# First projections as sums of three float32r products, four more places for the experts' weights, and a changed order of late loads

## What is computed

```python
sh1, sc1, g1, sh2, sc2, g2 = adaln_params(c, w_mod[l], b_mod[l])       # silu(c) @ w_mod + b_mod, in 12 parts of 512
hx = modulate(rms_norm(x, norm1_g[l]), sh1, sc1)                       # 512 tokens
hc = modulate(rms_norm(ctx, norm1_g[l]), csh1, csc1)                   # 256 context tokens
split(h @ w_in)  # q (512), f (512), b (512), v (512), gate, aq (512), ak and av (256), ...: the projections
...              # a gated recurrence over q, f, b, v in both directions; attention over aq, ak, av; mixing; x + g1 * y
aff = softmax(h @ w_router); gate, idx = top_k(aff.T, 64)              # each of 16 experts picks 64 tokens
hid = silu(h[idx] @ w_gate) * (h[idx] @ w_up); ye = (hid @ w_down) * gate
x = x + g2 * scatter_add(ye)
```

## Time and profile before

| | us |
|---|---|
| median of 3 runs | 1913.41 (1909.41 to 1919.11) |
| the profiled execution's own time | 1913.68 |
| its span, first to last instruction | 1912.4 |
| PE busy | 1721.0 (90%) |
| DVE busy | 796.1 (42%) |
| ACT busy | 570.9 (30%) |
| read from and written to DRAM | 322.83 MB and 4.20 MB |

### The profile page before, as it was taken

How to read it: one execution, slowest core, us unless ns; L and a number is a source line. 1 busy time by engine, 2 the same in 40 slices (tenths; PEclk the granted TensorE clock), 3 DMA queues, 4 the chain that set the end, 5 groups by cost and what they waited for, 6 DMA issues and landing times.

```text
span 1912.4 us, 20334 instructions
## 1 busy us (share of the span) xinstructions
PE 1721.0 (90%) x8150; PEld 1123.7 (59%) x8150; DVE 796.1 (42%) x1325; ACT 570.9 (30%) x1026; POOL 117.2 (6%) x123
## 2 busy tenths in 40 slices
PE   5989899886999996998888888999888899999999
PEld 2656667564877773333332333687544678888877
DVE  2164655456633432021120211547577434444444
ACT  2224563564343321110110100431544442222221
POOL 0002121012100001000000000000100001010010
PEclk9999899988999997999999999999999899999999
DMA  8221201123323267999999999443400122222301
GB/s 311 89 74 44 89 23 45 67 89 132 102 75 133 95 267 277 424 424 424 422 424 424 425 423 419 152 131 88 132 1 1 45 88 88 88 88 93 111 18 45
DMA packets 93185, 329.40 MB, mean 172 GB/s; under 512 B 7828, under 2 KB 22820, under 8 KB 68516
## 3 DMA queue, kind: packets, MB, share of 16 engines
q1 hardware_dynamic: 86032, 315.80, 42.6%
q10 hardware_dynamic: 5716, 8.05, 1.3%
q0 software_dynamic: 1344, 4.25, 0.6%
HBM read 322.83 MB, written 4.20 MB: 171 GB/s over the span
## 4 chain that ended last, share of the span: by engine, by line
PE 66%; DMA 16%; DVE 9%; ACT 6%; issue 2%; ACTq 0%; SPq 0%; DVEq 0%
PE PS L672 21%; PE PS L1061 9%; PE PS L815 8%; DMA room<-in_w_exp_up_dram 8%; PE PS L413 7%; DMA ring<-in_w_exp_gate_dram 6%; PE PS L409 3%; PE PS L544 3%; PE PS L626 3%; PE PS L888 2%; PE PS L469 1%; DMA ring<-in_w_in_dram 1%; PE PS L698 1%; PE PS L826 1%; PE PS L1003 1%
## 5 line engine op out<-in xcount | busy, mean ns | idle before, releaser
L1791 DVE TENSOR_TENSOR wR<-ring,wR 128x1024 fp32r<-128x1024 f32 (+2 forms) x134 | 151.4, 1130 | 223.3 <-ACT wR L1176 223.2
L1176 ACT CAST wR<-ring 128x1024 fp32r<-128x1024 f32 (+2 forms) x134 | 130.0, 971 | 203.5 <-PE PS L1061 126.5
L1061 PE MATMUL PS<-wR,hR 128*128 128x512 f32 x768 | 176.2, 390 | 8.9 <-DVE tmp L2571 6.9
L672 PE MATMUL PS<-xR,wR 128*128 128x512 f32 x768 | 175.6, 389 | 0.9 <-DVE wR L1791 0.9
L1061 PEld LDWEIGHTS PS<-wR,hR 128*128 128x128 f32 x768 | 143.5, 188 | 41.5 <-DVE tmp L2571 9.6
L672 PEld LDWEIGHTS PS<-xR,wR 128*128 128x128 f32 x768 | 144.0, 188 | 31.1 <-issue 1.3
L815 PE MATMUL PS<-room,xeT 128*64 128x512 f32 x512 | 115.7, 595 | 27.2 <-DMA room<-in_w_exp_up_dram 15.1
L672 PE MATMUL PS<-hR,wR 128*128 128x512 f32 x528 | 128.5, 405 | 8.2 <-DVE wR L1791 5.6
L815 PE MATMUL PS<-ring,xeT 128*64 128x512 f32 x512 | 117.4, 604 | 19.3 <-DMA ring<-in_w_exp_up_dram 15.8
L672 PEld LDWEIGHTS PS<-hR,wR 128*128 128x128 f32 x528 | 103.2, 197 | 34.3 <-issue 8.7
L672 PE MATMUL PS<-hR1h,wR 128*128 128x512 f32 x320 | 102.2, 394 | 2.4 <-DVE wR L1791 2.4
(11 more groups left out here) (469 smaller groups left out, 2628.7 us busy)
## 6 DMA issues: line engine op xcount, KB each, us to landing
ring<-in_w_exp_gate_dram SPq DMA_DIRECT2D x32, 1024.0 KB, 27.6
room<-in_w_exp_gate_dram SPq DMA_DIRECT2D x32, 1024.0 KB, 28.1
ring<-in_w_exp_up_dram SPq DMA_DIRECT2D x32, 1024.0 KB, 26.4
room<-in_w_exp_up_dram SPq DMA_DIRECT2D x32, 1024.0 KB, 27.4
ring<-in_w_exp_down_dram SPq DMA_DIRECT2D x32, 1024.0 KB, 26.5
room<-in_w_exp_down_dram SPq DMA_DIRECT2D x32, 1024.0 KB, 27.8
ring<-in_w_mod_dram SPq DMA_DIRECT2D x12, 2048.0 KB, 7.9
ring<-in_w_in_dram SPq DMA_DIRECT2D x11, 2048.0 KB, 9.3
```

The lines of the kernel that those rows point to most:

```text
L672: mm = T.matmul(b, o[s][:, k, :], x(t, k), start=(k == ks[0] and j == 0), stop=(k == ks[-1] and j == 2))
L1061: mm = T.matmul(down[m], uR[:, r % 2, s, k, 128 * i:128 * i + 128], o[t][:, 0, 512 * q:512 * q + 512], start=(k + j == 0), stop=(k == 3 an ...
L1176: A.copy(parts(wR, chunks, n)[0], W.view(unit)[:, ks, cs]).then_inc(act_hi.sem, act_hi.up(key))
L1791: V.tensor_tensor(lo, W.view(unit)[:, ks, cs], hi.bitcast(F32), ALU.subtract) \
```

## The change

It has two parts.

**First projections.** aq, akv, f, q and v of the first heads become sums of three float32r products (`token_terms`, `feature_terms`). The tokens get high and low terms (`hSt`, `hSc`: high, of tokens and context; `hSl`: low), the weights go through twelve chunks of 1024 words (`first_chunks`: aq 4, akv 2, f 2, q 2, v 2) with two pairs of buffers `wS`. aq and akv now run chunk by chunk over all their tiles (4 and 6 banks at once). A unit is free when its last chunk is subtracted, no longer when PE has used it. The ten small loads move from ACT to POOL. ACT and DVE take queries before keys, and parts of their order around `prepare(0)` move.

**Router and experts.** The normed tokens are stored in four pieces; the norm's root is a logarithm and an exponential; the first round of the top-64 reads PSUM instead of a copy; `gmat` is made after the first `up`; PE waits for two copies of `xeT` at a time. Nine rooms instead of eight, and three places that are used once, by units 7, 15 and 19 of the experts; units 18, 7 and 15 are loaded after the others of the first twenty: 18 after the store, 7 and 15 after the first gather.

```diff
+    ONCE = {7: "gathered", 15: "gathered", 19: "mixed"}
+            if k == 2 and n in self.ONCE:
+                slots = [NS + len(more) + list(self.ONCE).index(n)]
+                n += 1
+            elif k == 2:
+                if not cycle:
+                    cycle = [(at + j) % NS for j in range(NS)]
+                    cycle[4:4] = range(NS, NS + 4)
+                    cycle += range(NS + 4, NS + len(more))
+                slots = [cycle[turn % len(cycle)]]
...
+    def order(self):
+        first = self.number["gate", 0, 0, 0]
+        late = (18, 7, 15)
+        ahead = [n for n in range(20) if n not in late]
+        return [*range(first), *(first + n for n in (*ahead, *late)), *range(first + 20, len(self.units))]
...
+    more = [(what, rooms[r][:, i, :]) for what, r, i in (("xk", 0, 0), ("xk", 0, 1), ("uT", 1, 0), ("uT", 1, 1),
+                                                        ("mixed", 2, 0), ("mixed", 2, 1), ("mixed", 3, 0), ("mixed", 3, 1),
+                                                        ("strips", 1, 2))]
...
+        def token_terms(b, w, i, ks, start, stop):
+            for n, k in enumerate(ks):
+                for j, (s, t) in enumerate(TERMS):
+                    mm = T.matmul(b, hS(s, k, 128 * i, 128 * i + 128), w[t][:, n, :], ...)
...
         def qkv():
-            w = W.view("aq")
-            for i in range(4):
-                for k in range(8):
-                    mm = T.matmul(b, hT[:, k, 256 + 128 * i:384 + 128 * i], w[:, k, :], start=(k == 0), stop=(k == 7))
+            for n in range(4):
+                T.wait_ge(*dve_lo["aq", 2 * n])
+                for k in range(2 * n, 2 * n + 2):
+                    T.wait_ge(*dve_in["lx", k])
+                for i in range(4):
+                    mm = token_terms(bs[i], w, i + 2, range(2 * n, 2 * n + 2), n == 0, n == 3)
...
+        def prepare_first(pool):
+            for h in range(2):
+                T.wait_ge(*dve_lo["f0", h])
+                feature_terms(b[:, 0:512], w, 256, 768)
+                feature_terms(b[:, 512:768], w, 0, 256).then_inc(pe_scan.sem, pe_scan.up(("f", 0, h)))
+            yield
+            for h in range(2):
+                T.wait_ge(*dve_lo["q0", h])
+                feature_terms(b, parts(wS, first_chunks, 8 + h), 256, 768)
+                if h == 0:
+                    mod_product(pool, 4)
+            yield
+            mod_turn(pool, 4)
+            ...
...
-        zero = prepare(first, 0)
-        for n in range(6):
-            next(zero)
+        zero = prepare_first(first)
+        next(zero)
         turn_keys(rest)
...
             for k in range(1, 8, 2):          # ACT, setup
                 A.activation(hT[:, k, 256:768], bank(("hx", k)), ACT.Identity, ...)
+                A.copy(hSt[:, k - 1, :], hT[:, k - 1, 256:768]).then_inc(s.sem, s.up(("hi", k - 1)))
+                A.copy(hSt[:, k, :], hT[:, k, 256:768]).then_inc(s.sem, s.up(("hi", k)))
+                if k < 4:
+                    copy_hi(wS, first_chunks, k // 2)
...
+                for to, key in ((hT[:, k, 0:256], "hc"), (hSc[:, k, :], "hic")):
+                    A.activation(to, b, ACT.Identity, bias=modc[:, k, 1:2], scale=A1[:, 1, k:k + 1])
...
+            A.activation(spare, eps, ACT.Ln).then_inc(s.sem, s.up())          # ACT, router
-            A.activation(rinvc, ..., ACT.Sqrt, bias=eps, scale=1.0 / (32 * 1024))
+            inverse_root(rinvc, ..., 1.0 / (32 * 1024), s, "rms")
-            A.dma_start(h2d.rearrange("(t p) n -> p t n", p=128), h2k).then_inc(s_h2, 16)
+            for i in range(4):
+                for q in range(2):
+                    ...
+                A.dma_start(h2d[128 * i:128 * i + 128, :], h2k[:, i, :]).then_inc(s_h2, 16)
...
-            V.tensor_copy(aff, bank("aff")[0:64, 0:256]).then_inc(s.sem, s.up("aff"))
+                rs, left = slice(8 * r, 8 * r + 8), aff if r else bank("aff")[0:64, 0:256]
...
         gather(0)                             # POOL
+        gather(1)
+        G.wait_ge(*pe_moe["up", 0, 3])
         for k in range(8):
             G.tensor_scalar(gmat[:, k, :], ...)
...
-        for i, (name, sources, _, _) in enumerate(W.units):
+        for i in W.order():                   # SP
+            name, sources, _, _ = W.units[i]
+            if name == ("down", 0, 1, 0):
+                S.wait_ge(s_h2, 16 * 4)
```

More of the change, by code:

```diff
@@ L81, with __init__ @@
 class Ring:
-    def __init__(self, tensor, sems, units, more):
+    ONCE = {7: "gathered", 15: "gathered", 19: "mixed"}
+    def __init__(self, tensor, sems, units, more, once):
         self.tensor, self.sems, self.units = tensor, sems, units
-        self.places = [tensor[:, 2048 * i:2048 * i + 2048] for i in range(NS)] + [place for _, place in more]
+        self.places = [tensor[:, 2048 * i:2048 * i + 2048] for i in range(NS)] + [place for _, place in more] + once
         self.number = {u[0]: i for i, u in enumerate(units)}
         self.slots, self.value, self.before, self.free = [], [], [], {}
[L93 to L100, removed]
-            else:
-                size, top = 1 if k * n <= 2048 and k <= 4 else 2, 4 if 4 <= i < whole else NS
+        at, n, turn, count = 0, 0, 0, [0] * len(self.places)
+        holder = [None] * NS + [what for what, _ in more] + [self.ONCE[n] for n in self.ONCE]
+        whole, cycle = self.number["gate"], []
+        for i, (name, sources, k, width) in enumerate(units):
+            if k == 2 and n in self.ONCE:
[7 more added lines that the diff above has]
+                slots = [cycle[turn % len(cycle)]]
+                turn, n = turn + 1, n + 1
+            else:
+                if cycle:
+                    at, cycle = (at + turn % (NS + len(more))) % NS, []
+                size, top = 1 if k * width <= 2048 and k <= 4 else 2, 4 if 4 <= i < whole else NS
                 at = 0 if at + size > top or i == whole else at
@@ L396, in parts @@
         a, b = ks.stop - ks.start, cs.stop - cs.start
+        if chunks is first_chunks:
+            return [wS[2 * (n % 2) + x].rearrange("p (a b) -> p a b", b=b) for x in range(2)]
         at = (n + (chunks is not mix_chunks)) % 2
@@ L401, in done @@
         key = chunks[n][0]
+        if chunks is first_chunks:
+            return pe_in["used", n] if n < 6 else pe_scan[key[0][0], 0, key[1]]
         return pe_mm[key, 7 if key[0] == "down" and key[2] == 3 else 3 if key[-1] == 6 and key[0] in "q kv kw" else 0]
@@ L479, in qkv @@
                             mm.then_inc(pe_in.sem, pe_in.up(("hc", k)))
[L480 to L488, removed]
+            bs = []
+            for c in range(2):
+                T.wait_ge(*dve_lo["akv", c])
+                w = parts(wS, first_chunks, 4 + c)
+                if c == 0:
+                    T.wait_ge(*dve_in["lc", 7])
+                for i in range(6):
+                    if c == 0:
+                        bs.append(pool.take(T, ("akv", i), act_in["av", i]))
+                    mm = token_terms(bs[i][:, 0:256], w, i, range(4 * c, 4 * c + 4), c == 0, c == 1)
+                    if c == 1:
+                        mm.then_inc(pe_in.sem, pe_in.up(("akv", i)))
+                if c == 0:
+                    mm.then_inc(pe_in.sem, pe_in.up(("used", 4)))
+                else:
+                    pe_in.also(("used", 5))
         def turn_keys(pool):
@@ L806, in pair_product @@
                     units = [(name, p, kq, e2) for e2 in range(2)]
-                    if name == "gate" and kq % 2 == 0:
-                        T.wait_ge(*act_moe["xe", p, kq // 2])
+                    if name == "gate":
+                        T.wait_ge(*act_moe["xeT", p, kq])
                     for u in units:
@@ L1996, in prepare @@
             yield
+            if q == 0:
+                sub_lo(wS, first_chunks, 11)
             if r:
@@ L2628, in dve @@
         zero = prepare(0)
-        for n in range(8):
+        for n in range(6):
             next(zero)
@@ L2693, in pool @@
         G.tensor_tensor(AB[:, 1, :], colA[:, 32:40], colA[:, 40:48], ALU.mult).then_inc(pool_moe.sem, pool_moe.up("gmat"))
-        for p in range(1, 8):
+        for p in range(2, 8):
             gather(p)
```

222 lines of the change are left out of this document (153 added, 69 removed).

## The result

The changed kernel takes **1888.12 us** (median of 4 runs, 1879.09 to 1890.92) against 1914.12 beside it (4 runs), a ratio of 0.9856 with an interval of 0.9813 to 0.9898. The forecast was 1887 with a range of 1877 to 1899. Taken again later (x5), it gave 1887.15 (6 runs, 1880.11 to 1894.58) against 1913.05: 0.9854 (0.9827 to 0.9882). x5 also asked whether the parts add up as their totals do (then 1897) or as the stages of the profiles do (then 1888): it was 1887. The profiled execution after took 1886.63 us, 1.3 over its span.

The account below looks back on a forecast made before the run. It took PE to bound the first projections and DMA transfers the experts. From 1913.7 us it subtracted 16.3 (projections), 9.9 (places) and 0.5 (router) to forecast 1887, with an 8-in-10 range of 1877 to 1899.

Parts of the forecast that it names:

- Products, -18.3: First projections: three float32r products replace each float32 one, PE work falling from 103.3 to 85.0 us, a gain of 18.3.
- q's load and the slow clock, -8.5; keys, +3.4: Before q: hidden load saves 5.3 us and slow clock 3.2; the keys' turns and copy wait, now exposed, cost 3.4.
- v, +1.2: End of first projections: v's load lands later, then cast and subtraction, only partly covered by PE work; 1.2 us lost.
- The start, +3.3: Ahead of aq: ACT and DVE must first split tokens and weights, so aq starts at 42.7 instead of 39.36; 3.3 lost.
- Clock at the start, +2.6: At aq's start: PE's 4.1 us of idleness lowers the granted clock; 2.6 us lost, bounds nothing and 3.2.
- Places, -9.9: Experts: twenty units placed before the first freed place instead of sixteen; four loads of 2.47 us leave the full stretch, -9.9.
- the middle rival: Experts don't gain: gather and stream start later in one queue, or PE is the bound; 1897 us, chance 0.12.
- Router, -0.5: Router's chain: a copy saves 0.4 us, fewer xeT waits 0.8, unit 18 beside the gather costs 0.7, root 0; -0.5.
- What follows moves along unchanged: After v: recurrence and attention have their loads earlier than before and shift along unchanged; no time added or saved.
- splitting uncovered: First projections: four or five chunks behind aq wait for cast and subtraction, 10 us in all; 1897 us, chance 0.13.
- handoffs at a low clock: First projections: all twelve chunks expose 2.3 us each and the clock falls to a mean of 0.8; 1928 us, chance 0.03.
- the better case (1882): First projections: no clock fall at the start, and half the stalls at keys and v; 1882 us, chance 0.07.

Follow-up runs that it names:

- x8: Changed kernel with 30 identity turns ahead of aq, mod 4's product before the keys' turns, and 36 turns during the first gather's wait; 1881.05 us, ratio 0.9823.
- x4: Kernel before, all float32, with only q's first unit sent to places 4 and 5 so its load needn't wait for PE; 1905.54 us, ratio 0.9965.
- x10: Changed kernel without the third product of each sum in the first projections, all casts and subtractions kept; 1873.25 us, ratio 0.979.
- x1: Kernel before with only the first projections' part of the change; 1899.0 us, ratio 0.992.
- x6: Changed kernel with 30 turns of the identity on PE ahead of aq; 1884.95 us, ratio 0.9853.
- x11: Changed kernel with the experts' units loaded in listed order and SP not waiting for the store; 1910.01 us, ratio 0.9992.
- x2: Kernel before with only the router and experts part of the change, projections in float32; 1909.92 us, ratio 0.9981.
- x9: Kernel before with only the twenty places, their order of loads and the move of gmat; 1910.67 us, ratio 0.998.
- x7: Changed kernel with mod 4's product moved from between q's halves to ahead of the keys' turns; 1882.97 us, ratio 0.9838.
- x3: Changed kernel with sixteen places, loads in listed order and no wait for the store; 1897.52 us, ratio 0.9918.
- x12: Kernel before with 16 identity turns added ahead of aq; 1913.17 us against 1916.17, ratio 0.9988.

## Why the prediction was right

The total came out within 1.2 us of the forecast, and the profiled sum (-27.1 against -26.7) too. By its steps:

- **Products, -18.3.** Right. In x8, at the full clock, 48 matmuls of 512 columns take 11.28 us, 0.235 each; v's 72 of 256 columns take 8.53, 0.118 each. Added up from the chains, with each slow stretch at its full-clock length (6.87 of x4 for q's first half before, 11.28 of x8 for the first 48 and 5.5 for q's first half after), the products took 103.8 us before and 84.5 after: 19.3. The splitting is hidden: the only wait for `wS` is the first (x10 shows how near the others were).
- **q's load and the slow clock, -8.5; keys, +3.4.** Right in sum. The load is hidden. From f's end (102.25) to q's start (105.75) pass 3.5 us, of them 2.39 a wait. x4 alone gave -6.2. Not predicted was a second fall of the clock behind the keys: q's first half took 6.73 instead of 5.5, 1.2 us.
- **v, +1.2.** Measured 1.02, and by the mechanism named: the wait is for mod 4's row on ACT, behind v's cast. 0.38 of it was there before, so it adds 0.6.
- **The start, +3.3.** Measured 3.2, by a near tie of two mechanisms. The prediction summed ACT's and DVE's lists and passed over aq's own load, which lands at 39.31 before, just ahead of the first product, and at 40.18 after; cast (1.05) and subtraction (1.24) follow it. But ACT's list was through at 40.04, 0.14 us ahead of it, and in x1, x5, x6, x8, x10 and x11 the load lands first (38.96 to 39.56) and the list is the last, as predicted. Without the later landing the list would have set the start, 0.14 us sooner.
- **Clock at the start, +2.6.** It fell, as forecast. Size 1.7 us in the kernel after (12.94 against 11.28), 2.5 in x5 (13.75).
- **Sum of part 1, -16.3.** v's end moved by 17.5 (15.4 in x5, 16.6 in x1). The measured terms (-19.3 - 8.5 + 3.5 + 1.2 + 0.6 + 3.2 + 1.7) give -17.6.
- **Places, -9.9.** Measured -9.9, and 10 to 11 in every pair. The full stretch was read as ten slices where the earlier trace rows have nine; no term rests on it. That unit 18 shares the gather's time was right, but the price was too low: the gather takes 5.57 us instead of 4.42 (5.5 to 5.7 in all kernels with unit 18 there, 4.2 to 4.5 in the others), 1.2 for the 0.7 taken. That the store is covered by 2 to 3 us was wrong. Its 5 us were 7.7 even in the kernel before (issued at 720.63), and 8.6 for the last piece after; it landed at 714.66, 0.3 us ahead of the indices, and the gather started some 0.25 late for it. In x2, x9 and x10 it landed behind them, which the prediction had named as a sign of being wrong. x11 shows the queue that the middle rival feared, where the order is left out.
- **Router, -0.5.** Measured -0.6 to the first freed place, in part by luck. The parts are: the copy -0.4, the two copies of `xeT` -0.7 (0.82 instead of 1.51), the gather +1.2, its late start +0.2, together +0.3. The other -0.9 are a clock that came back sooner: the first products ran at 0.50 from 738.2 to 742.7 before and from 723.3 to 725.9 after. The prediction has no term for it. For the root the row, with its table load of 1283 ns, was right, and the rule of the Trainium skill ("ScalarE: Activation LUTs", "Table sets: the hidden batching unit") did not hold here: a table load of 1.28 us stands between logarithm and exponential at 696.68.
- **"What follows moves along unchanged".** The step that was thinnest. The unchanged middle took 2.3 us more, the rest 1.4 less, and in the parts alone up to 5 more. It cancelled here by luck, and that the total came within 1.2 us is luck too: the same kernel's runs reach from 1879.09 to 1894.58.

The rivals: splitting uncovered and handoffs at a low clock did not come; the places did gain; the better case (1882) lies inside the runs' spread, and x7 and x8 reach it on purpose.

## What to carry to other kernels

When an engine's work is made cheaper, price the next late item at each handoff before counting the saving: here the start, two short waits and two falls of the clock behind them gave back 10.6 of 27.8 us (3.2 + 3.5 + 1.0, and 1.7 + 1.2 for the clock), and moving one ready product into the gap (x7) won 3 of them again. Loads whose places come free at different times belong in the queue in the order in which they come free: the same four places gain 10 us that way, and in the order of use the kernel with them (x11) is 12 us slower than the one without (x3). Check such an order against every other transfer that must land in time: here the store that the first gather needs came 0.3 to 2 us too late behind the added loads. Compare small gains by stages with fixed marks, since unchanged stages of this kernel moved by as much as the part under test.

## What was not expected of the hardware

- A wait of 2.62 us on PE was followed by a clock of 0.50 for 3 to 7 us in eleven kernels and by 1.00 in three (before, x7, x11), in before and x12 with the same instructions on PE around it. With a wait of some 4 us at the start the clock fell in the kernel after, x1, x5 and x7; with 30 identity turns in it (x6, x8) it stayed at 1.00.
- The gather of 0.5 MB took 4.2 to 4.5 us alone and 5.5 to 5.7 beside one load of 1024 KB.
- The store of 2.1 MB took 2.9 us for its last piece with no load of the experts under way (x11) and 8.6 to 10.3 behind five loads of 1024 KB.
- Stages whose code was the same in all kernels differed by up to 7 us (502.5 to 509.4) and 11 us (733.6 to 744.7) between profiled executions. In the last stage the mean granted clock went along: 0.98 in the shortest (x4), 0.97 in after, 0.96 in the longest (x5).
